# Layer norms of a two-block transformer kernel: the residual written into PSUM, the normalised tile transposed, x made later

## The reference

```python
for l in range(DEPTH):                      # DEPTH = 2, ALPHA = (2 * DEPTH) ** 0.25
    x = layer_norm(ALPHA * x + 0.5 * swiglu(x, ffn1_w_gate[l], ffn1_w_up[l], ffn1_w_down[l]),
                   ln_g[l, 0], ln_b[l, 0])
    proj = x @ w_in[l]
    ...                                     # pooling, gated convolution, neighbourhood attention -> y
    x = layer_norm(ALPHA * x + y @ w_out, ln_g[l, 1], ln_b[l, 1])
    x = layer_norm(ALPHA * x + 0.5 * swiglu(x, ffn2_w_gate[l], ffn2_w_up[l], ffn2_w_down[l]),
                   ln_g[l, 2], ln_b[l, 2])
```

## Time and profile before

| | |
|---|---|
| median of 3 runs | 2997.88 us (2996.47 to 3000.35) |
| the profiled execution | 2998.23 us |
| its span, first to last instruction | 2996.4 us |
| mean granted TensorE clock | 0.965 of full |

### The profile page before, as it was taken

One profiled execution on the slowest core, in us unless ns is written; L12 is line 12 of the kernel. 1 busy time (PEld: TensorE's weight loads), 2 busy tenths in 40 slices (PEclk: granted clock), 3 DMA queues, 4 the chain that ended last, 5 costly groups with the idle time before them and its releaser, 6 DMA issues.

```text
span 2996.4 us, 51984 instructions
## 1 busy us (share of the span) xinstructions
PE 2800.4 (93%) x21700; PEld 2593.2 (87%) x21700; DVE 1592.4 (53%) x2184; ACT 1293.3 (43%) x1832; POOL 477.8 (16%) x199
## 2 busy tenths in 40 slices
PE   7999999999999999988889899999998878989998
PEld 7988899898889989987779788999988778888898
DVE  5566555656655565543545515555564274552555
ACT  3435443443543443444523454444444452344433
POOL 0000000000000000034423660000004451474000
PEclk9999999999999999998999999999999899999999
DMA  8755466675536646632322544665663331244563
GB/s 233 209 157 161 120 183 188 170 210 156 160 114 188 183 143 187 197 99 87 104 65 72 165 152 133 184 187 160 186 187 95 92 113 51 103 149 123 162 188 126
DMA packets 622827, 445.08 MB, mean 149 GB/s; under 512 B 27904, under 2 KB 589344, under 8 KB 622176
## 3 DMA queue, kind: packets, MB, share of 16 engines
q1 hardware_dynamic: 622688, 443.09, 49.8%
HBM read 441.99 MB, written 1.05 MB: 148 GB/s over the span
## 4 chain that ended last, share of the span: by engine, by line
PE 86%; DVE 9%; ACT 3%; issue 1%; DMA 0%; POOL 0%; SPq 0%; ACTq 0%; DVEq 0%; POOLq 0%
PE ps L373 19%; PE ps L374 18%; PE ps L375 18%; PE ps L389 7%; PE ps L390 7%; PE ps L391 7%; PE ps L630 1%; PE ps L606 1%; PE ps L1353 1%; ACT w_hi L645 1%; PE ps L1160 1%; PE ps L1061 1%; PE ps L1343 1%; DVE zT L1495 1%; DVE moments L908 1%
## 5 line engine op out<-in xcount | busy, mean ns | idle before, releaser
L373 PE MATMUL ps<-in_hi,w_hi 128*128 128x256 f32 x4352 | 1263.2, 290 | 69.5 <-POOL w_lo L814 31.1
L645 ACT ACTIVATE w_hi<-raw 128x1024 fp32r<-128x1024 f32 x800 | 844.9, 1057 | 947.1 <-PE ps L375 626.4
L374 PE MATMUL ps<-in_lo,w_hi 128*128 128x256 f32 x4352 | 1248.4, 287 | 0.0
L375 PE MATMUL ps<-in_hi,w_lo 128*128 128x256 f32 x4352 | 1247.6, 287 | 0.0
L814 DVE TENSOR_TENSOR w_lo<-raw,w_hi 128x1024 fp32r<-128x1024 f32 x606 | 742.7, 1226 | 742.8 <-ACT w_hi L645 741.7
L373 PEld LDWEIGHTS ps<-in_hi,w_hi 128*128 128x128 f32 x4352 | 852.9, 196 | 89.8 <-issue 32.4
L374 PEld LDWEIGHTS ps<-in_lo,w_hi 128*128 128x128 f32 x4352 | 852.9, 196 | 7.3 <-issue 0.5
L375 PEld LDWEIGHTS ps<-in_hi,w_lo 128*128 128x128 f32 x4352 | 851.9, 196 | 0.0
L814 POOL TENSOR_TENSOR w_lo<-raw,w_hi 128x1024 fp32r<-128x1024 f32 x194 | 477.2, 2468 | 2270.5 <-ACT w_hi L645 2269.7
L389 PE MATMUL ps<-w_hi,hid_hi 128*128 128x512 f32 x704 | 276.0, 392 | 0.0
L390 PE MATMUL ps<-w_lo,hid_hi 128*128 128x512 f32 x704 | 275.9, 392 | 0.0
(11 more groups left out here) (302 smaller groups left out, 2665.8 us busy)
## 6 DMA issues: line engine op xcount, KB each, us to landing
raw<-in_w_ffn_in SPq DMA_DIRECT2D x176, 512.0 KB, 3.8
raw<-in_w_mix SPq DMA_DIRECT2D x112, 512.0 KB, 3.8
raw<-in_ffn_w_gate SPq DMA_DIRECT2D x88, 512.0 KB, 4.1
raw<-in_ffn_w_up SPq DMA_DIRECT2D x88, 512.0 KB, 3.8
raw<-in_ffn_w_down SPq DMA_DIRECT2D x88, 512.0 KB, 3.6
raw<-in_w_ffn_out SPq DMA_DIRECT2D x88, 512.0 KB, 3.4
raw<-in_w_in SPq DMA_DIRECT2D x40, 512.0 KB, 3.8
raw<-in_w_out SPq DMA_DIRECT2D x32, 512.0 KB, 3.5
```

The lines of the kernel that those rows point to most:

```text
L373: nc.tensor.matmul(o, lh, rh, start=first, stop=False, **kw)
L374: nc.tensor.matmul(o, lh, rl, start=False, stop=False, **kw)
L375: return nc.tensor.matmul(o, ll, rh, start=False, stop=last, **kw)
L645: nc.scalar.activation(w_hi[:, e % SPLIT, :], raw[:, e % RAW, :], ACT.Copy).then_inc(sem("split_high"), 1)
```

## The change

In the first block, TensorE opens banks 0 to 3 once with eight matmuls on ones, so that later matmuls without `start` add onto what another engine wrote there. Before each feed-forward's down product, 2*ALPHA*x is written into those banks: in layer 0's first feed-forward by ScalarE from `x_tok` (`act_seed`), in the other three by VectorE straight from the norm's input (`dve_ln_seed`, with a bias doubled beforehand by `dve_double_bias`). The down product adds onto it (`seeds`), so norms 0 and 2 take their statistics from the banks and need no addition; norm 1 keeps it.

Between norm and product, the tile (z - mean)/std is made in four quarters into `n_tok`, three by ScalarE (Identity with per-partition scale and shift) and one by VectorE, and is transposed into banks 4 to 7. Behind the transpose VectorE applies gain and bias, now one number per partition (`dve_ln_turn`, from the new tile `ln_cols`), into `xT`; ScalarE rounds from `xT`. x itself, where it is needed later (after norm 0, and after the last norm), is made by `dve_ln_x`; after norm 0 among the low parts of the input projection. After norms 1 and 2 the seeds take its place. Warm-up matmuls are 4, 10, 4 (12 in layer 1) in place of 15 each. Gate and up of the feed-forwards use banks 4 and 5 in place of 7 and 4; the turns of the second block go to banks 4 to 7 but for one. SyncE issues one load more (`ln_cols`), issues the bias strips from tile 5 on in place of 3, and in layer 1 waits there for the seeds.

The diff, cut to its core:

```diff
+        tok_shift = sb("tok_shift", [P, HALF])
+        tok_twice = sb("tok_twice", [P, HALF])
+        ln_cols = sb("ln_cols", [P, LAYERS, 3, 2, KD])
...
+        n_tok = yT[:, :, :].rearrange("p k t -> p (k t)").rearrange("p (a d) -> p a d", a=HALF)
+        xT = sq[:, :, :]
...
+        WARM_BANK = 7
+        TURN_BANK = 4
...
+        def pe_ln_turn(pe, n):
+
+            q = turn0 + n - 1
+            pe.wait_ge(sem("ln_act"), 3 * q + 1)
+            turn_four(n_tok, 0, 0, TURN_BANK)
+            pe.wait_ge(sem("ln_vec"), q + 1)
+            turn_four(n_tok, 1, 0, TURN_BANK)
+            pe.wait_ge(sem("ln_act"), 3 * q + 2)
+            turn_four(n_tok, 0, 1, TURN_BANK)
+            pe.wait_ge(sem("ln_act"), 3 * q + 3)
+            turn_four(n_tok, 1, 1, TURN_BANK)
 
...
-        FFN_BANK = (7, 4)
-
-        def pe_ffn(pe, n, e0, chunk):
+        FFN_BANK = (4, 5)
+
+        def pe_ffn(pe, n, e0, chunk, seeds=None):
...
-                    mm = three_rows(b, e, hid_hi[:, j % 2, :], hid_lo[:, j % 2, :], j == 0, last)
+                    if seeds is not None and j == 0 and b % 2 == 0:
+
+                        pe.wait_ge(sem("seeded"), HALF * seeds + b // 2 + 1)
+                    mm = three_rows(b, e, hid_hi[:, j % 2, :], hid_lo[:, j % 2, :], j == 0 and seeds is None, last,
+                                    skip_group_check=seeds is not None)
...
+        def act_ln_turn(act, n):
+
+            for c in range(KD // 2):
+                act.wait_ge(sem("ln_turned"), 4 * (turn0 + n - 1) + c + 1)
+                two = slice(2 * c, 2 * c + 2)
+                nc.scalar.activation(in_hi[:, two, :], xT[:, two, :], ACT.Copy).then_inc(sem("in_high"), 1)
...
+
+            def root(t):
                 act.wait_ge(sem("tok_stat"), HALF * (norm0 + n) + t + 1)
                 nc.scalar.activation(tok_std[:, t:t + 1], mean_var[:, t, 1:2], ACT.Sqrt, bias=cst(eps, 1))\
                     .then_inc(sem("tok_std"), 1)
+
+            def normed(t, d):
+
+                act.wait_ge(sem("ln_scale"), HALF * (norm0 + n) + t + 1)
+                nc.scalar.activation(n_tok[:, t, d * 512:(d + 1) * 512], ln_in(n, t, d), ACT.Identity,
+                                     scale=tok_rstd[:, t:t + 1], bias=tok_shift[:, t:t + 1]).then_inc(sem("ln_act"), 1)
+
+            root(0)
+            if turn:
+                normed(0, 0)
+            root(1)
+            if turn:
+                normed(0, 1)
+                normed(1, 1)
+
...
+        def ln_in(n, t, d):
+
+            return z_tok[:, t, d * 512:(d + 1) * 512] if n == 1 else ps[:, 2 * t + d, :]
...
+        def act_seed(act, s):
+
+            act.wait_ge(sem("opened"), 1)
+            for t in range(HALF):
+                nc.scalar.activation(ps[:, 2 * t:2 * t + 2, :].rearrange("p b c -> p (b c)"), x_tok[:, t, :], ACT.Copy,
+                                     scale=2 * ALPHA).then_inc(sem("seeded"), 1)
...
+        def dve_ln_turn(dve, steps, n, chunk, gain, bias):
+
+            for c in range(KD // 2 + 1):
+                if c < KD // 2:
+                    dve.wait_ge(sem("turned"), 4 * (turn0 + n) + c + 1)
+                    for k in (2 * c, 2 * c + 1):
+                        ins = nc.vector.tensor_scalar(xT[:, k, :], two_tiles(TURN_BANK + c)[:, k - 2 * c, :], gain(k), bias(k),
+                                                      ALU.mult, ALU.add)
+                    ins.then_inc(sem("ln_turned"), 1)
+                if c:
+                    dve.wait_ge(sem("ln_turned"), 4 * (turn0 + n - 1) + c)
+                    dve.wait_ge(sem("in_high"), chunk + c)
+                    two = slice(2 * c - 2, 2 * c)
+                    nc.vector.tensor_tensor(in_lo[:, two, :], xT[:, two, :], in_hi[:, two, :].bitcast(F32), ALU.subtract)\
+                        .then_inc(sem("in_ready"), 1)
...
+                if e == 2 and up is None and whole is None:
+                    second_seed()
...
-        def dve_ln(dve, steps, n, alpha, ready, turn=True):
+        def dve_ln(dve, steps, n, ready, turn=True):
 
             half = [slice(d * 512, (d + 1) * 512) for d in range(2)]
             for t in range(HALF):
                 for d in range(2):
                     ready(2 * t + d)
-                    steps.link(nc.vector.scalar_tensor_tensor(z_tok[:, t, half[d]], x_tok[:, t, half[d]], alpha,
-                                                              ps[:, 2 * t + d, :], ALU.mult, ALU.add))
-                    ins = nc.vector.bn_stats(moments[:, t, d, :], z_tok[:, t, half[d]])
+                    if n == 1:
+                        steps.link(nc.vector.scalar_tensor_tensor(z_tok[:, t, half[d]], x_tok[:, t, half[d]], ALPHA,
+                                                                  ps[:, 2 * t + d, :], ALU.mult, ALU.add))
+                    ins = nc.vector.bn_stats(moments[:, t, d, :], ln_in(n, t, d))
                 steps.link(ins)
                 nc.vector.bn_aggr(mean_var[:, t, :], moments[:, t, :, :].rearrange("p a b -> p (a b)"))\
                     .then_inc(sem("tok_stat"), 1)
-            dve.wait_ge(sem("tok_stat"), HALF * (norm0 + n + 1))
-
-            def scaled(t, d):
-
-                return steps.mark(nc.vector.scalar_tensor_tensor(z_tok[:, t, half[d]], z_tok[:, t, half[d]], mean_var[:, t, 0:1],
-                                                                 ln_gain[n][:, half[d]], ALU.subtract, ALU.mult))
-
-            done = [scaled(t, 0) for t in range(HALF)]
-            dve.wait_ge(sem("tok_std"), HALF * (norm0 + n + 1))
-            steps.link(nc.vector.reciprocal(tok_rstd[:, :], tok_std[:, :]))
+                if t == 0:
+                    continue
+                for u in range(HALF):
+                    dve.wait_ge(sem("tok_std"), HALF * (norm0 + n) + u + 1)
+                    steps.link(nc.vector.reciprocal(tok_rstd[:, u:u + 1], tok_std[:, u:u + 1]))
+                    nc.vector.scalar_tensor_tensor(tok_shift[:, u:u + 1], mean_var[:, u, 0:1], -1.0, tok_rstd[:, u:u + 1],
+                                                   ALU.mult, ALU.mult).then_inc(sem("ln_scale"), 1)
+            dve.wait_ge(sem("ln_scale"), HALF * (norm0 + n + 1))
+            if turn:
+                nc.vector.tensor_scalar(n_tok[:, 1, half[0]], ln_in(n, 1, 0), mean_var[:, 1, 0:1], tok_rstd[:, 1:2],
+                                        ALU.subtract, ALU.mult).then_inc(sem("ln_vec"), 1)
+
+        def dve_ln_x(dve, steps, n, t):
+
+            half = [slice(d * 512, (d + 1) * 512) for d in range(2)]
+            done = [steps.mark(nc.vector.scalar_tensor_tensor(z_tok[:, t, half[d]], ln_in(n, t, d), mean_var[:, t, 0:1],
+                                                              ln_gain[n][:, half[d]], ALU.subtract, ALU.mult))
+                    for d in range(2)]
             for d in range(2):
-                for t in range(HALF):
-                    steps.need(done[t])
-                    ins = nc.vector.scalar_tensor_tensor(x_tok[:, t, half[d]], z_tok[:, t, half[d]], tok_rstd[:, t:t + 1],
-                                                         ln_bias[n][:, half[d]], ALU.mult, ALU.add)
-                    if turn:
-                        ins.then_inc(sem("turn_in"), 1)
-                    elif d:
-                        ins.then_inc(sem("x_ready"), 1)
-                if d == 0:
-                    done = [scaled(t, 1) for t in range(HALF)]
+                steps.need(done[d])
+                ins = nc.vector.scalar_tensor_tensor(x_tok[:, t, half[d]], z_tok[:, t, half[d]], tok_rstd[:, t:t + 1],
+                                                     ln_bias[n][:, half[d]], ALU.mult, ALU.add)
+            return ins
+
+        def dve_ln_seed(dve, steps, n, t):
+
+            half = [slice(d * 512, (d + 1) * 512) for d in range(2)]
+            if t == 0:
+                steps.link(nc.vector.tensor_scalar(tok_twice[:, :], tok_rstd[:, :], 2 * ALPHA, None, ALU.mult))
+            done = [steps.mark(nc.vector.scalar_tensor_tensor(z_tok[:, t, half[d]], ln_in(n, t, d), mean_var[:, t, 0:1],
+                                                              ln_gain[n][:, half[d]], ALU.subtract, ALU.mult))
+                    for d in range(2)]
+            for d in range(2):
+                steps.need(done[d])
+                ins = nc.vector.scalar_tensor_tensor(ps[:, 2 * t + d, :], z_tok[:, t, half[d]], tok_twice[:, t:t + 1],
+                                                     ln_bias[n][:, half[d]], ALU.mult, ALU.add)
+            ins.then_inc(sem("seeded"), 1)
+
+        def dve_double_bias(dve, steps, n):
+
+            steps.link(nc.vector.tensor_scalar(ln_bias[n], ln_bias[n], 2 * ALPHA, None, ALU.mult))
...
-                pe_turn(pe, 0, x_tok, BY_COLUMNS, waits=l > 0)
-                pe_ffn(pe, 0, E1_FFN1, C1_FFN1)
-                pe_warm(pe, 15)
-                pe_turn(pe, 1, x_tok, BY_COLUMNS)
+                if l == 0:
+                    for b in range(4):
+                        for d in range(2):
```

(73 more changed lines are left out.)

69 lines of the change are left out of this document (37 added, 32 removed).

## The result

The changed kernel takes 2979.89 us (median of 4 runs, 2979.07 to 2980.75) beside 2998.97 us for the kernel before on the same chip (4 runs, 2996.47 to 3000.35): ratio 0.9938, 95% interval 0.9923 to 0.9952, 0.62% faster. Its profiled execution has a span of 2977.3 us, 19.1 less than the 2996.4 of before.

What follows compares the result with a forecast made beforehand. TensorE, busy 93%, was taken to bound the kernel, losing time at the norms. From 2998.2 us, parts 1 to 3 (11.2 + 5.5 - 0.35) took 16.4 and part 4 added 1.4: 2983.2, said as 2983, range 2972 to 2994.

Steps and rivals of the forecast that it cites:

- Part 1: Four norms behind a feed-forward: residual additions leave, statistics read PSUM at no charge; saves 2.79 us each, 11.2 in all.
- Part 2: Five norms, second aggregation (A) to next stage's first product (P): shorter path, P = A + 5.6 or 6.0; saves 5.5 us.
- Rival 1: Between norm and product: ScalarE-VectorE hand-overs eat part 2, only the additions count; 2989 us, chance 0.20.
- Part 3: Last norm, which turns nothing: small steps and ScalarE's second root come first, so the first scaled tile is 0.35 us later.
- The clock: Five restarts behind norms: same clock picture as before, so nothing charged, +-1.3 us at each.
- Rival 2: Restarts slower for want of warm-ups, 1.3 us more at five, transposes at half clock; 2991 us, chance 0.12.
- rival 5: Norms and restarts: the chain was too pessimistic and restarts run at full clock; 2975 us, chance 0.08.
- Part 4: Stages behind norms: VectorE's moved x and seed groups mostly covered; costs 0.4 us (half clock) to 3.6 (full), taken 1.4.
- The doubling: Doubling of the bias before layer 0's last norm, within part 4: adds 0.4 us.
- Rival 3: Moved groups not covered: PSUM writes at double price put five second groups 2.7 us late each; 2996.5 us, chance 0.10.
- Rival 4: Turning norms: ScalarE's Identity outside the square root's table, fifteen table loads add 19.2 us; 3002 us, chance 0.05.

Runs made afterwards that it cites:

- before_filled: Kernel before, first block's norm gaps filled: 18 warm-ups in place of 15, 3 more between transposes, 23 in the last norm; 2990.27 us, ratio 0.9968.
- warm_fit: Changed kernel with 8, 14, 8 and 18 warm-ups in place of 4, 10, 4 and 12; 2984.87 us, ratio 0.9943.
- warm0: Changed kernel without the warm-up matmuls ahead of the first block's norm transposes; 2984.12 us, ratio 0.9941 to the kernel before.
- best: Changed kernel with norm gaps and two attention waits filled, layer 1's pad clearing and the bias doubling moved late into the feed-forward; 2980.82 us, ratio 0.9928.
- x_pool: Changed kernel with x behind norm 0 made on GpSimd in place of VectorE's two groups in the input projection; 2988.74 us, ratio 0.9963.
- seed_pool: Changed kernel with GpSimd making x behind all five turning norms, ScalarE writing it into the banks for three feed-forwards; 2997.59 us, ratio 0.9995.
- no_seeds_all: Changed kernel without seeding (additions back, x made into SBUF), warm-ups 14, 14, 14 and 24, two attention waits filled; 2986.75 us, ratio 0.9957.
- warm15: Changed kernel with fifteen warm-ups in every gap in place of 4, 10, 4 and 12; 2985.48 us, ratio 0.9949.
- before_all: Kernel before with norm gaps filled by warm-ups and two TensorE waits in the attention filled too; 2985.42 us, ratio 0.9957.
- fit_att: Changed kernel with norm gaps filled (8, 14, 8 and 18 warm-ups) and two attention waits filled; 2979.70 us, ratio 0.9932.
- no_seeds: Changed kernel without seeding: additions back in norms behind both feed-forwards, x made into SBUF, bias not doubled; 2995.05 us, ratio 0.9974.

## Why the prediction was right

The range and the direction held, and parts 1 and 2 held as mechanisms. That the time came within 3 us of the forecast is in part luck: two terms that were wrong by 10.6 and 5.6 us stood against each other.

- **Part 1** (11.2 us): measured 2.88, 2.87, 2.88 and 2.87 at the four norms, 11.5. The statistics read from PSUM at no extra cost (minimum, median, maximum ns of L988 by source, and of the other two instructions below):

```profile
L988 DVE BATCH_NORM_STATS2 moments<-ps x16: 644/681/693, 208.0 to 1042.4; 128x6 f32<-128x512 f32 x16
L988 DVE BATCH_NORM_STATS2 moments<-zT x8: 693/694/696, 326.2 to 845.7; 128x6 f32<-128x512 f32 x8
...
L1026 DVE SCALAR_TENSOR_TENSOR ps<-zT,tok_twice,arena x12: 751/754/755, 343.5 to 865.6; 128x512 f32<-128x512 f32 x12
...
L1012 DVE SCALAR_TENSOR_TENSOR x_tok<-zT,tok_rstd,arena x12: 740/743/747, 222.6 to 1048.7; 128x512 f32<-128x512 f32 x12
```

  The Trainium skill's table (VectorE: DVE Perf Modes, section on the TRN2 errata), which the prediction weighed, would have them 0.26 us longer per norm; measured they are 0.013 us shorter each. By the measurement, that rule does not hold for these instructions.
- **Part 2** (5.5 us): as the two traces stand, P - A fell by 0.87, 1.04, 1.74, 1.01 and 1.73, 6.4 us. Part of that is clock, since slow transposes lay in the old path. Between `before_filled` and `warm_fit`, both at full clock, it is 0.74, 1.04, 1.98, 0.74 and 1.06: 5.6. The chain of steps held in its parts as well: ScalarE's pass 0.77 from PSUM and 0.80 from SBUF against 0.80, P at A + 5.84 and 5.76 against 5.6 and 6.0. Rival 1 is out. Behind P the first 48 matmuls are 0.6 us slower in all than in `before_filled`, as the chunks now come through two engines.
- **Part 3** (-0.35): -0.49.
- **The clock** (nothing, +-1.3 a restart): this step failed. The gaps of before lose 11.86 us when filled, those of after 1.21, so the change brought 10.65 by clock. The prediction saw the fall at one restart (0.68) and took the others for like it; they were at 0.50 to 0.57. The clock cost the six gaps 1.1, 1.5, 1.6, 2.1, 2.4 and 3.2 us (before less `before_filled`), and only the first is within the 1.3. It then compared the time from the last warm-up to P, 5.4 against 5.6, and called it the same picture. The 5.6 is a slip: with A at 210.96, P = A + 5.6 is 216.6, and the stretch 6.4, as measured (210.09 to 216.53). So by the prediction's own yardstick the new stretch is longer, and it holds more idle time (1.90, 0.76 and 1.59 us against 1.30 and 1.33), and yet the clock held: the yardstick doesn't tell. That idle time in the gap costs clock is shown (`warm0`, `before_filled`); why the changed gaps keep it with these waits is not. Rival 2 had the sign wrong; rival 5 had the clock right, though not its other half, since the chain from A to P was not too pessimistic.
- **Part 4** (0.4 to 3.6, taken 1.4): measured 6.98. That it is VectorE's work shows in what ends the stops (L874 and L1026, both VectorE), and in `best`, where 1.7 us of that work moved elsewhere at full clock gave back 1.73. `x_pool` and `seed_pool`, without the groups, fit it, but behind slow restarts. It is not the clock by itself: `before_filled` has fast restarts and no tail. The choice within the range failed first: at full clock the forecast's own count was 3.6 (its five terms of 0.6 and the 0.4 add up to 3.4). The size failed next: 1.05 in each input projection and 1.15 in layer 1's feed-forward, where 0.6 was counted; of these 0.69 are left in a feed-forward without seeds (`no_seeds_all`), and the rest fits the wait of the down product for the seeds of banks 2 and 3 (0.39 us at 351.03, 0.38 in the other two), which the prediction had said would not be there. The doubling is 0.46 (0.4 forecast). The third norm's feed-forward took 2.15, because the two memsets (0.51 and 0.49 us), booked as a gain in part 2 for moving behind the turn, only moved into the next full stretch; `best` gets 1.25 of this back by moving them on.
- **Rival 3** was right that the moved groups are not covered, at 7.0 of its 13.5 us, but its reason is void: writing PSUM costs VectorE 754 ns where SBUF costs 743. **Rival 4** is void: no load stands between L798 and L804. Where ScalarE does load a table, behind the second norm, its next instruction starts 1.30 us behind the load's start (334.00 to 335.30), so no drain is seen on top of the load's 1.28.

Summed as the prediction sums: 11.5 + 5.6 - 0.5 - 0.6 = 16.0 of gaps at full clock, plus 10.65 of clock, less 6.98 of stages, less 0.5 elsewhere: 19.2, beside a measured 19.1. The forecast had 16.4 - 1.4 = 15.0.

What stays open: when exactly the clock falls. Every kernel whose gaps were filled so that no wait of TensorE ahead of or within the transposes was over 0.8 us read 1.00 throughout them (`warm15` but for a wait of 1.46 in its last gap, `warm_fit`, `before_filled`, `before_all`, `no_seeds_all`, `fit_att` and `best`). The kernel before fell in all six gaps, in five with two waits of 1.30 to 1.39 and 1.33, in the last with one of 3.83. But the changed kernel held in four gaps with waits of 1.9 and 2.2 and fell in the two with 1.99 and 2.75, and like gaps of `no_seeds` went both ways. Nor was it tested whether transposes count as work in the way that products do; the time since the last warm-up alone doesn't tell either, since 5.4 us of it fell before the change and 6.4 held after. The gaps were seen in one execution of each kernel. Nor is it known what the second block's 1 to 4 us from kernel to kernel are.

## What to carry to other kernels

Price the clock at every restart by its own row, not at one, and try first what it costs to fill TensorE's waits with dummy products: here other counts and one inserted group of three gave 9.6 us by the medians, where the change gave 19, without touching the norm. Work moved off a critical path must be laid against the stretch where it lands at the speed that the change itself brings: faster products took away the cover, and what was saved between A and P at equal clocks (4.94 us) was paid back in the stages behind (5.20), so only the seeds, which removed additions from the path, were a net gain (9.2 us by the columns, 7.5 by the ratios). When stages not touched vary by several microseconds, cut the traces at common events and compare stage by stage.

## What the runs showed of the hardware

- Matmuls add onto what ScalarE or VectorE wrote into a bank that was opened once by matmuls, at no cost seen in the products: the first of each three takes a mean of 393 ns in the feed-forwards (L394), and 392 in the kernel before (L389).
- VectorE's scaling by two per-partition numbers takes 0.81 us for 128x512 from PSUM and 0.55 from SBUF, while centring and gain (three operands, one of them from SBUF) takes 0.743 from PSUM and 0.746 from SBUF: the source's price depends on the instruction.

```profile
L1001 DVE TENSOR_SCALAR yT<-ps,mean_var,tok_rstd x3: 809/809/811, 212.5 to 727.9; 128x512 f32<-128x512 f32 x3
L1001 DVE TENSOR_SCALAR yT<-zT,mean_var,tok_rstd x2: 545/546/546, 333.0 to 848.3; 128x512 f32<-128x512 f32 x2
...
L1007 DVE SCALAR_TENSOR_TENSOR zT<-ps,mean_var,arena x12: 740/743/752, 221.3 to 1047.3; 128x512 f32<-128x512 f32 x12
L1021 DVE SCALAR_TENSOR_TENSOR zT<-zT,mean_var,arena x8: 743/746/752, 342.2 to 864.2; 128x512 f32<-128x512 f32 x8
```

- A GpSimd instruction over two SBUF tiles holds a VectorE subtraction over two SBUF tiles until it ends (2.57 us in place of 0.68), and in the first block, where VectorE makes every low part, that makes GpSimd no place for spare work near a restart: the five gaps of `seed_pool` in which it worked got 4.2 to 4.5 us longer.
